# The first conditioning group laid out by columns and finished two feature tiles at a time between four weight chunks

## What is computed

```python
def _adaln(cond, w, b):
    m = jax.nn.silu(cond) @ w + b
    return [t[:, None, :] for t in jnp.split(m, 6, axis=-1)]

m_ctx = _adaln(c_ctx[None, :], ada_w[l], ada_b[l])
m_lat = _adaln(c, ada_w[l], ada_b[l])
hp = _rms(xp, norm_mix[l]) * (1.0 + m_ctx[1]) + m_ctx[0]
hs = _rms(xs, norm_mix[l]) * (1.0 + m_lat[1]) + m_lat[0]
z = h @ w_in          # both token groups; the first 416 columns are q_lat, ckv, kpe
```

## Time and profile before

| | |
|---|---|
| median of 3 runs | 1518.42 us (1518.38 to 1523.59) |
| profiled execution, its own time | 1517.46 us |
| its span, first to last instruction | 1515.7 us |
| PE busy | 1473.4 us, 97% of the span |
| DMA | 469.08 MB, mean 309 GB/s |

### The profile page before, as it was taken

The page is one execution under the profiler, slowest core; times in us unless marked ns, Lnnn a source line. Parts: engine busy times, 40 slices in busy tenths (PEclk is TensorE's granted clock), DMA queues, the critical chain, the costliest instruction groups (busy, mean ns, idle before and its releaser), DMA issues.

```text
span 1515.7 us, 20328 instructions
## 1 busy us (share of the span) xinstructions
PE 1473.4 (97%) x8326; PEld 1241.7 (82%) x8326; DVE 1184.2 (78%) x1163; ACT 967.9 (64%) x986; POOL 27.8 (2%) x29
## 2 busy tenths in 40 slices
PE   5989999999999999999999999999999999999997
PEld 2868899998977888888888888888888888888885
DVE  2555754445897788999979899889889888988996
ACT  2455543343458497777777767787777777776773
POOL 0110000000000200000000000000000000000000
PEclk9999999999999999999999999999999999999999
DMA  9676776656743579999989999989999998999993
GB/s 375 232 281 250 243 255 225 222 178 220 265 172 112 195 281 374 374 360 370 376 318 374 372 358 371 374 334 358 376 373 358 372 375 317 374 372 357 373 374 137
DMA packets 100914, 469.08 MB, mean 309 GB/s; under 512 B 8108, under 2 KB 38972, under 8 KB 51664
## 3 DMA queue, kind: packets, MB, share of 16 engines
q1 hardware_dynamic: 99408, 464.81, 81.7%
q10 hardware_dynamic: 864, 1.76, 0.3%
q0 software_dynamic: 544, 1.15, 0.2%
HBM read 466.55 MB, written 1.14 MB: 309 GB/s over the span
## 4 chain that ended last, share of the span: by engine, by line
PE 91%; DVE 4%; DMA 3%; ACT 1%; issue 1%; POOL 0%; SPq 0%; ACTq 0%; DVEq 0%; POOLq 0%
PE bank L1568 20%; PE bank L1567 20%; PE bank L1566 20%; PE bank L1572 6%; PE bank L1574 5%; PE bank L1573 5%; DMA raw<-ada_w 2%; PE bank L1583 2%; PE bank L2075 2%; PE bank L1914 1%; PE bank L1868 1%; PE bank L1869 1%; PE bank L1870 1%; DVE hid L1290 1%; PE bank L2040 1%; PE bank L1600 1%
## 5 line engine op out<-in xcount | busy, mean ns | idle before, releaser
L1450 DVE TENSOR_TENSOR low<-raw,high 128x2048 fp32r<-128x2048 f32 x333 | 749.3, 2288 | 101.2 <-ACT high L807 99.2
L807 ACT ACTIVATE high<-raw 128x2048 fp32r<-128x2048 f32 x333 | 630.1, 1922 | 91.1 <-DMA raw<-moe 89.7
L1566 PE MATMUL bank<-high,hidH 128*128 128x512 f32 x896 | 350.1, 391 | 0.0
L1568 PE MATMUL bank<-high,hidL 128*128 128x512 f32 x896 | 349.2, 390 | 0.0
L1567 PE MATMUL bank<-low,hidH 128*128 128x512 f32 x896 | 348.7, 389 | 0.0
L1572 PE MATMUL bank<-hidH,high 128*128 128x256 f32 x736 | 210.9, 287 | 4.0 <-DVE hidL L945 3.3
L1573 PE MATMUL bank<-hidL,high 128*128 128x256 f32 x736 | 208.1, 283 | 0.0
L1574 PE MATMUL bank<-hidH,low 128*128 128x256 f32 x736 | 208.1, 283 | 0.0
L1568 PEld LDWEIGHTS bank<-high,hidL 128*128 128x128 f32 x896 | 168.2, 188 | 35.0
L902 DVE TENSOR_TENSOR low<-raw,high 128x2048 fp32r<-128x2048 f32 (+2 forms) x59 | 133.9, 2278 | 80.4 <-ACT high L502 80.3
L1566 PEld LDWEIGHTS bank<-high,hidH 128*128 128x128 f32 x896 | 168.2, 188 | 34.5
(11 more groups left out here) (225 smaller groups left out, 1338.2 us busy)
## 6 DMA issues: line engine op xcount, KB each, us to landing
raw<-moe SPq DMA_DIRECT2D x336, 1024.0 KB, 4.9
raw<-ada_w SPq DMA_DIRECT2D x48, 1024.0 KB, 6.7
raw<-ffn_gu SPq DMA_DIRECT2D x44, 512.0 KB, 5.1
raw<-ffn_down SPq DMA_DIRECT2D x11, 1024.0 KB, 5.1
raw<-w_in SPq DMA_DIRECT2D x8, 1024.0 KB, 10.4
raw<-conv_pw SPq DMA_DIRECT2D x16, 512.0 KB, 5.6
raw<-w_o SPq DMA_DIRECT2D x4, 1024.0 KB, 6.2
raw<-conv_pw SPq DMA_DIRECT2D x4, 1024.0 KB, 6.2
```

Source lines behind the costliest of these rows:

```text
L807: a.activation(high[:, m % SPLITS, :], raw[:, n % RAWS, :], ACT.Copy).then_inc(S("high_ready"), 1)
L1450: v.tensor_tensor(low[:, n % RAWS, :], raw[:, n % RAWS, :], high[:, m % SPLITS, :].bitcast(F32), ALU.subtract).then_inc(S("low_ready"), 1)
L1566: pe.matmul(out, xh, wh, start=start, stop=False)
L1568: return pe.matmul(out, xl, wh, start=False, stop=stop)
```

## The change

The constants get two more columns, the weights of group 0 are stored in a new order, x moves to SP's queue ahead of all pieces, and the order of pieces is new:

```diff
-    ada(0, 0, 5)
-    order.append(("win", 0, 0))
-    ada(0, 5, 8)
-    order.extend([("win", 0, 1), ("win", 2, 0), ("win", 2, 1)])
+    for q, piece in enumerate((("win", 0, 0), ("win", 2, 0), ("win", 0, 1), ("win", 2, 1))):
+        ada(0, 2 * q, 2 * q + 2)
+        order.append(piece)
...
+            for h in range(2):
+                sp.dma_start(xT[:, h * KH:(h + 1) * KH, :], t["x"][:, h * KH:(h + 1) * KH, :]).then_inc(S(f"x_in{h}"), 16)
...
+    first = inp["ada_w"][0][:, 0:2 * D].reshape(2, 4, P, 2, 4, 2 * P).transpose(4, 0, 2, 1, 3, 5)
+    arrays["ada_first"] = np.ascontiguousarray(first.reshape(KT, P, PIECE))
```

Pieces 2q and 2q+1 of group 0 now hold all 1024 input features for shift and scale of feature tiles 2q and 2q+1 alone. So after two pieces two tiles of `hid` can be finished. PE's side:

```diff
+            def first_piece(q, h):
+                m = STREAM[("ada", 0, 2 * q + h)]
+                pe.wait_ge(S(f"raw_in{m % RAWS}"), arrived_value(m))
+                if h == 0 and q >= 2:
+                    pe.wait_ge(S("first_rows"), q - 1)
+                for c in range(GC):
+                    last = pe.matmul(bank[32 * c:32 * c + 32, (6, 3)[q % 2], :], cond[:, KH * h + c, :],
+                                     raw[:, m % RAWS, c * 512:(c + 1) * 512], start=h == 0, stop=h == 1)
+                last.then_inc(S("direct_used"), 1)
...
+            def first_sum(q):
...
+                if q:
+                    pe.wait_ge(S("aff0_ready"), q)
+                for j in range(4):
+                    last = pe.matmul(bank[:, 2, j * P:(j + 1) * P].rearrange("p (r c) -> p r c", c=TILES),
+                                     ada4[:, j * P:(j + 1) * P],
...
-            ada_sum(0)
-            spare(3, 0, 9)
...
+            first_piece(1, 0)
+            chunk(("win", 0, 0), 0, pairs_of(0), split_ready(0), False, {}, 0, {1: pair_between(1, 1, True)})
+            spare(7, 0, 8)
+            first_piece(2, 0)
+            spare(7, 0, 8)
+            chunk(("win", 2, 0), 0, pairs_of(4), None, False, {}, 0, {1: pair_between(2, 1, False)})
+            first_sum(2)
+            spare(7, 0, 8)
+            first_piece(3, 0)
+            chunk(("win", 0, 1), 4, pairs_of(0), split_ready(0), False, {(1, KH - 1): "zq_product"}, 0,
+                  {1: pair_between(3, 1, True)})
+            spare(7, 0, 8)
```

`pair_between(q, 1, True)` runs `first_piece(q, 1)` and then `first_sum(q)` in the middle of a chunk, behind its first two feature tiles. `first_sum(q)` waits for DVE's copy of the rows. The second broadcast moves from behind the second quarter of the fourth chunk to behind the third. DVE's side, once for each q:

```diff
+            def first_hidden(q, between=None):
+                first_rows(q)
+                first_out(q)
+                for k in (2 * q, 2 * q + 1):
+                    modulate_context(0, k)
+                if between:
+                    named(*between)
+                for k in (2 * q, 2 * q + 1):
+                    hidden_low(0, k)
...
-            named("win", 0, 0)
-            rows_out(0)
-            mod_out(0)
-            gain_scale(0)
-            modulate_split(0, {1: ("win", 0, 1)})
+            first_hidden(0, ("win", 0, 0))
+            first_hidden(1)
             named("win", 2, 0)
+            first_hidden(2)
+            named("win", 0, 1)
+            first_hidden(3)
             named("win", 2, 1)
```

More of the change, by code:

```diff
@@ L933, in gain_scale, with first_rows, first_out @@
                       "aff_ready")
+            def first_rows(q):
+                v.wait_ge(S("direct_used"), DNUM[("ada", 0, 2 * q + 1)] + 1)
+                if q:
+                    v.wait_ge(S("first_summed"), q)
+                st.mark(v.tensor_copy(ada4[:, :], bank[:, (6, 3)[q % 2], :]), "first_rows" if q < 3 else "ada4_ready")
+            def first_out(q):
+                v.wait_ge(S("first_summed" if q < 3 else "ada_summed"), q + 1 if q < 3 else 1)
+                src = bank[:, 2, :].rearrange("p (w j r c) -> p w j r c", w=2, j=2, c=TILES)[:, :, :, 0, :]
+                b0 = COLS["ada_b"][0]
+                bias = par[:, b0:b0 + 2 * KT].rearrange("p (w k) -> p w k", w=2)[:, :, 2 * q:2 * q + 2]
+                st.do(v.tensor_tensor(mod[:, 0, 0:2, 2 * q:2 * q + 2, :], src,
+                                      bias.unsqueeze(3).to_broadcast([P, 2, 2, TILES]), ALU.add),
+                      "first_out" if q < 2 else "ada_out")
+                g0 = COLS["gain"][0] + 2 * q
+                st.do(v.scalar_tensor_tensor(aff[:, 2 * q:2 * q + 2, :], mod[:, 0, 1, 2 * q:2 * q + 2, :], 1.0,
+                                             par[:, g0:g0 + 2].unsqueeze(2).to_broadcast([P, 2, TILES]), ALU.add,
+                                             ALU.mult), "aff0_ready")
             def modulate_context(i, k):
@@ L954, in modulate_split @@
                         modulate_context(i, k)
-                    if i and p < 3:
+                    if p < 3:
                         scaled(i, p + 1)
@@ L1647, in chunk @@
                                  kk == starts and c0 == 0, kk == (starts - 1) % KT and c0 > 0)
-                    if by_tile and (m, k) in after:
+                    if (m, k) in after:
                         st.mark(last, after[m, k])
@@ L1651, in chunk @@
                         between[m]()
+                    if not by_tile and m == 3 and k in between:
+                        between[k]()
                 last.then_inc(S("piece_used"), 1)
@@ L1676, in pairs_of @@
             def pairs_of(b0):
                 return lambda m: (b0 + m // 2, (m % 2) * TOK)
[L1679 to L1690, removed]
+            def pair_between(q, h, summed):
+                def run():
+                    first_piece(q, h)
+                    if summed:
+                        first_sum(q)
+                return run
@@ new lines, in _, with latent_sums @@
+            spare(7, 0, 8)
+            def latent_sums():
+                lsq = heads_sq[:, 0].rearrange("p h d -> p (h d)")
+                pe.wait_ge(S("lat_sq"), 2)
+                tile_sums(lsq[:, 0:TOK], 7, 0, True, False)
+                tile_sums(lsq[:, TOK:2 * TOK], 7, 0, False, False)
+                st.mark(tile_sums(lsq[:, 2 * TOK:3 * TOK], 7, TOK, False, True), "lat_sum")
+            chunk(("win", 2, 1), 4, pairs_of(4), None, True, {}, 0,
+                  {0: latent_sums, 2: lambda: broadcast(7, 0, LAT_C, 4, 2)})
```

67 lines of the change are left out of this document (40 added, 27 removed).

## The result

The changed kernel takes 1531.45 us (median of 4 runs, 1530.25 to 1532.21), the kernel before in the same series 1518.71: ratio 1.008, interval 1.0067 to 1.0094. It is slower by 12.7 us. In a second series, against its own runs of before: 1532.14 against 1518.57, ratio 1.009 (1.0065 to 1.0114). The profiled execution of the changed kernel took 1530.25 us, span 1528.5, 12.8 more than the profiled one of before.

A forecast was written before the change was run, and what follows sets the result against it. PE, full behind its idle start, was taken as the bound: -11.8 (start) +13.7 (added work) +8.2 (waits) = +10.1, transposes at 75.3 instead of 65.2 us, median 1528.5 us, range 1523 to 1533.5.

The forecast's parts named there:

- its own band of +8 to +12: The forecast's main case for the whole kernel, slower by 8 to 12 us; chance 0.50.
- the clock rival: PE at the slow clock through the first half-chunk, costing 5.0 us together: +15, 1533.5 us; chance 0.18.
- A, start of the first chunk: Kernel start: x lands earlier, so the first chunk starts at 24.9 us instead of 36.68, 11.8 us earlier.
- B, added work: Among the chunks: five pieces (5.0), three sums of rows (2.9) and spare products (5.9) add 13.7 us on PE.
- C, waits among the chunks: PE idles 3.4 us twice inside chunks and 2.2 before the third; less 0.83 before, 8.2 us more.
- clock: Sum's assumption from the start through the chunks: pauses behind the rise leave PE at the fast level, so nothing is added.
- No later stage has slack: Behind the chunks: whatever is late at 104 us is late at the end, as PE is nearly always busy.
- the two signs by which the prediction called itself wrong: Transposes before 71 us, or later stages giving part of the shift back.
- x late: Start: x not early as queues share the engines; first chunk some 6 us later, time near 1534; chance 0.04.
- Partly covered waits: Waits among the chunks partly hidden by x sooner, overlapping copy or quicker series: +4 to +7.6, about 1524.5 us; chance 0.22.
- Faster: Stream no longer holds PE behind the chunks, and part C's waits vanish: 1514.6 us; chance of any gain 0.06.
- a lower bound: Part C's waits not under 2.5 + 2.5 where copy and sum overlap other work: 4 us less.

The follow-up runs named there:

- Moving one series away: Changed kernel with the second pair (second piece and its sum of rows) moved ahead of the first chunk, rows copied by ACT: 1523.99 us, ratio 1.0040.
- the kernel without spares and waits: Changed kernel, second pair ahead of the first chunk, win 0,1 split ahead of the third pair's series, 32 spare products among the chunks removed: 1518.94 us, ratio 1.0000.
- the kernel with filled waits: Changed kernel with spare products put in PE's pauses, all but the one ahead of the third chunk: 1528.66 us, ratio 1.0069.
- the last kernels: Column layout with every pair taken out of the waits, without and with w_qb requested directly behind win 2,1: 1514.34 and 1513.87 us, ratios 0.9962 and 0.9967.
- x first alone: Kernel before with only x moved to SP's queue ahead of the pieces: 1519.73 us, ratio 1.0015.
- all pauses filled: Changed kernel with spare products in every pause, also ahead of the third chunk: 1529.69 us, ratio 1.0071; again 1528.97 us, ratio 1.0062.
- the start filled: Changed kernel with spare products only in the two pauses ahead of the first chunk: 1532.16 us, ratio 1.0087.
- three pairs ahead: Column layout with every pair taken out of the waits, ACT copying, spare products only ahead of the first chunk: 1514.34 us, ratio 0.9962 to the kernel before.
- `qb` sooner: Kernel with every pair taken out of the waits, w_qb requested directly behind win 2,1 instead of behind three pieces of group 1: 1513.87 us, ratio 0.9967.

## Why the prediction was right, and where it was off

The direction and the range (1523 to 1533.5) held, and the three terms that made the forecast are in the trace. The size is less good than that: the median of 1531.45 is 2.95 over the 1528.5 of the forecast and outside its own band of +8 to +12, and nearer to the 1533.5 of the clock rival. At the transposes the forecast was +10.1 us, measured +14.75. Term by term, from the spacings of the rows above:

| term | forecast | measured |
|---|---|---|
| A, start of the first chunk | -11.8 | 26.15 - 36.68 = -10.5 |
| B, added work | +13.7 | the rest of the sum: +13.4 |
| C, waits among the chunks | +8.2 | 3.4 + 3.3 + 1.9 - 0.8 = +7.8 |
| clock | 0 | 2.5 + 1.55 = +4.05 |

**A, the start: right in kind, 1.3 us short.** ACT squared x at 6.65 and 8.36 instead of 5.8 and 7.8. Its row on the parameters just ahead stands at 6.52, only 0.5 us sooner than before, where drawing the rate of 0.42 MB per us back from 7.05 made it 1.2. The first sum of squares was at 10.81 instead of 9.8. Part of that is a slip in the sum: the prediction names the 0.50 for the rotary table, but 7.8 + 0.6 + 2 x 0.69 doesn't hold it. DVE's timeline has its additions directly behind it:

```profile
8.83 0.50 DVE L1069 TENSOR_TENSOR rope_tab<-const,par 128x32 f32<-128x32 f32 x4 [7.69 <-DMA const<-table]
9.25 1.41 DVE L1035 TENSOR_TENSOR hid<-hid 128x512 f32<-128x512 f32 x2
```

From there to the first chunk it is 15.3 us, forecast 15.1; in it are 0.4 for the sum of rows at half clock.

**B, the added work: right as a sum in this kernel.** The table's 13.4 is what the other terms leave. Added up from the starts of PE's rows it is 13.2: five pieces at 1.0, three sums at 0.9 to 0.95, and spares of 7.3 less the 1.95 of before; the prediction had counted each block of spares with its tail. What the term did not say is that its parts are no price list: the 32 spares take 7.3 us of PE, but without them the transposes come only 2.5 earlier where waits and a slow stretch follow, and the median falls by 4.0 where two shorter waits do.

**C, the waits: right.** The 3.4 and 3.3 are the spacing of the rows less 1.95 for piece and sum; by the idle column of the profile it is 3.0 each (0.82 + 2.19, 0.81 + 2.19), since that counts the tails as busy. From the piece to the second half of the first chunk 5.32 us, forecast 5.3 (27.8 to 33.1); in the third chunk 5.23; before the third chunk 5.78 from the sum's start, forecast 6.1. Moving one series away gave 6.9 us at the transposes: its 3.4, the clock's 2.5 in that half-chunk, and the piece's 1.0, which goes into a wait; its sum leaves the chunk and starts it as much later. `w_qb`, for which the prediction had 0.4 us of cover, cost a wait of 0.17.

**The clock: the term that was mis-sized.** I set it to zero because short pauses behind the rise had left the piece at 1.06 in the earlier trace rows. The step that failed is this inference from a pause of 1.42 us to pauses of 3.2 and 1.9. Measured: half clock from 21.5 on, behind the pause of 17.7 to 20.9, and again from 65.9 on, 0.3 us behind the end of one of 2.19. The length of a pause alone doesn't decide it: the 3.2 and 2.2 of the kernel without spares and waits brought no fall in its profile, the 1.95 of the kernel with filled waits brought one. Of the 5.0 us rival's parts, the half-chunk lost its 2.5 and the sum of rows 0.4; second sum and broadcast, ahead of the fall, were fast (1.17 and 0.71), and the slow piece at 22.36 (1.94) cost nothing, since PE waited for `hidL` anyway. A fall in the third chunk nobody had foreseen. The Trainium skill, TensorE: Matmul & The Clock Gate, section on HAM oscillation, says that a wait between groups of products can send the array back to half its clock; the trace agrees that it can, and filling the pauses took the slow stretches away (full clock from 16.8 to 100 us in two profiles).

**"No later stage has slack": off by 2 us.** This is one of the two signs by which the prediction called itself wrong, and it came, small as it is. The text ahead of the prediction says that the first 36 us hold most of PE's idle time; by the earlier trace rows they hold 18.2 of 42.3 us, and 18.3 lie behind 104.5. Of 14.75 us, 12.8 reach the end. 1.1 comes back at the landing of a piece of group 1 (6.18 to 5.08), the transfers behind it give some 0.4 (5.39 to 5.11 for the one of w_in), and one step of 0.7 near 365 us goes with a wait that only the kernel before has there. From PE's waits in the kernel before, between 250 and 370 us:

```profile
PE bank L1868 <- DVE upL L1250: 0.5, 1, 0.5
```

Why DVE is late there in one kernel and not in the other was not tried. The give-back of 2.0, and 0.7 less work and waits than forecast, offset half of the clock's 4.05 and the start's 1.3, and so the difference of the medians is 12.7 where 10.1 was forecast. That the errors have opposite signs is luck.

**The rivals.** Clock down: it was, in part, beside the forecast's mechanism and not in its place. x late: no. Partly covered waits: no, PE stood in each one at full length. Faster: not in this order; but the mechanism that I had called a lower bound (copy and sum overlapping other work) is what the last kernels do, and with the spares gone from among the chunks it turns the sign. They need no earlier stream for that; only with the transposes at 59 us does the stream become the bound.

## What to carry to other kernels

Cutting a long reduction into small ones lets the first product start earlier, but each small one has a latency across the engines (here 5.3 us from its last piece to the next product, with PE at work for 1.95 of them); put it behind work that is already ready, one stage ahead of its use, or the head start is paid back once for each. Filler products are free only in a wait. Where the next product is ready, count them as work; where they fill a pause, their price is nothing and their gain is the clock. When the front gets shorter, look at once for the next transfer in the ring: it was requested for the old pace.

## What was not expected of the hardware

- **Same kernel, other falls.** In two profiles of the changed kernel the half clock came at 21.5 to 31.8 and 65.9 to 69.3, and at 22.7 to 29.5, 36.3 to 39.7 and 67.1 to 70.5. With the first two pauses filled it came at 34.0 to 40.8 alone. Pauses of 3.2 and 2.2 us brought none in the kernel without spares and waits; a single one of 1.95 us brought one 1.1 us behind its end. What decides between them stays open.
- **The mean clock goes with the spread.** Of ten runs with x first alone, six at .995 to .996 took 1517.6 to 1519.8 us, four at .992 to .994 took 1522.0 to 1522.9.
- **The rise differs, too.** In the changed kernel and its variants, with the same instructions on PE ahead, it came at 14.5 to 16.9 us, worth up to 0.9 us at the second sum of squares.
- **Two rates of the experts.** 243.54 us between the rows of 32 products in most profiles, 244.11 in both of the kernel with all pauses filled, in that with the start filled and in that with three pairs ahead, with PE never idle. The kernel with `qb` sooner has the same products in the same order as the last of these and 243.56 and 243.54. In its stretch before (526.69 to 764.95) it has 238.26, where kernels at the faster rate have 237.5 and those at the slower one 238.1: so the rate changed within one execution. It isn't the list of products alone; the cause stays open, and some 2 us hang on it.
